# Attention stages of a two-block fp32 transformer kernel: units three deep, four gate products moved, twelve gate products per layer pair in split form

## The reference, cut to what matters

```
ga, gb, gc = the last three 1024-wide column groups of n @ w_in[i]
merged = (sigmoid(ga) * (ya @ w_branch[i, 0])
          + sigmoid(gb) * (yb @ w_branch[i, 1])
          + sigmoid(gc) * (yc @ w_branch[i, 2]))
h = h + merged @ w_out[i]
```

## Time and profile before

| | us |
|---|---|
| median of 3 runs | 3007.83 (3001.94 to 3012.53) |
| profiled execution, its own time | 3003.04 |
| its span | 3001.3 |
| PE busy | 2910.9 (97%) |
| DVE busy | 1695.5 (56%) |
| ACT busy | 1188.8 (40%) |
| mean granted PE clock | 0.983 |

### The profile page before, as it was taken

One profiled execution on the slowest core, in us unless ns is written; L12 is line 12 of the kernel. 1 busy time (PEld: TensorE's weight loads), 2 busy tenths in 40 slices (PEclk: granted clock), 3 DMA queues, 4 the chain that ended last, 5 costly groups with the idle time before them and its releaser, 6 DMA issues.

```text
span 3001.3 us, 49531 instructions
## 1 busy us (share of the span) xinstructions
PE 2910.9 (97%) x21376; PEld 2741.8 (91%) x21376; DVE 1695.5 (56%) x2824; ACT 1188.8 (40%) x1771; POOL 12.6 (0%) x20
## 2 busy tenths in 40 slices
PE   8999999999998999999999998999989999899998
PEld 8998788999998878899999996789989999678998
DVE  5666543665666553466666444456656654454665
ACT  5535422444445432244444233234454432332444
POOL 0000000000000000000000000000000000000000
PEclk9999999999999999999999898999999999999999
DMA  7544385555544344455664642445545565234553
GB/s 246 177 152 123 111 205 168 169 179 186 183 158 148 100 140 154 154 183 176 193 200 155 184 129 71 108 163 183 182 156 183 172 181 143 85 99 148 183 182 110
DMA packets 481273, 474.41 MB, mean 158 GB/s; under 512 B 47104, under 2 KB 464416, under 8 KB 480928
## 3 DMA queue, kind: packets, MB, share of 16 engines
q1 hardware_dynamic: 477472, 460.75, 49.2%
q0 software_dynamic: 3584, 10.49, 1.6%
HBM read 464.91 MB, written 6.29 MB: 157 GB/s over the span
## 4 chain that ended last, share of the span: by engine, by line
PE 92%; DVE 4%; ACT 3%; issue 1%; DMA 0%; DVEq 0%; ACTq 0%; SPq 0%
PE ps L829 33%; PE ps L928 32%; PE ps L949 17%; PE ps L982 4%; PE ps L1052 2%; PE ps L1022 1%; DVE WL L1676 1%; ACT WH L1349 1%; PE ps L872 1%; PE ps L876 1%; PE ps L880 1%; ACT REGION L1318 0%; PE ps L860 0%; DVE REGION L1819 0%; ACT L1335 0%
## 5 line engine op out<-in xcount | busy, mean ns | idle before, releaser
L1676 DVE TENSOR_TENSOR WL<-RAW,WH 128x2048 fp32r<-128x2048 f32 (+1 forms) x350 | 780.5, 2235 | 483.7 <-ACT WH L1349 481.6
L1349 ACT ACTIVATE WH<-RAW 128x2048 fp32r<-128x2048 f32 (+1 forms) x350 | 647.2, 1860 | 138.1 <-DMA RAW<-in_w_in 53.8
L949 PE MATMUL ps<-HH,WL 128*128 128x256 f32 x1408 | 394.8, 280 | 0.0
L949 PE MATMUL ps<-HH,WH 128*128 128x256 f32 x1408 | 394.3, 280 | 0.0
L949 PE MATMUL ps<-HL,WH 128*128 128x256 f32 x1408 | 394.0, 280 | 0.0
L928 PE MATMUL ps<-UH,WH 128*128 128x256 f32 x2688 | 378.5, 283 | 0.5 <-DVE WL L1676 0.5
L928 PE MATMUL ps<-UH,WL 128*128 128x256 f32 x2688 | 377.3, 283 | 0.0
L928 PE MATMUL ps<-UL,WH 128*128 128x256 f32 x2688 | 376.4, 282 | 0.0
L928 PEld LDWEIGHTS ps<-UH,WH 128*128 128x128 f32 x2688 | 346.2, 190 | 1.1 <-DVE WL L1676 0.7
L928 PEld LDWEIGHTS ps<-UL,WH 128*128 128x128 f32 x2688 | 346.7, 191 | 0.0
L928 PEld LDWEIGHTS ps<-UH,WL 128*128 128x128 f32 x2688 | 346.2, 190 | 0.0
(11 more groups left out here) (269 smaller groups left out, 3159.9 us busy)
## 6 DMA issues: line engine op xcount, KB each, us to landing
RAW<-in_w_ffn_in SPq DMA_DIRECT2D x88, 1024.0 KB, 5.1
RAW<-in_ffn_wi SPq DMA_DIRECT2D x88, 1024.0 KB, 5.1
RAW<-in_w_in SPq DMA_DIRECT2D x86, 1024.0 KB, 5.3
RAW<-in_w_ffn_out SPq DMA_DIRECT2D x32, 1024.0 KB, 5.1
RAW<-in_ffn_wo SPq DMA_DIRECT2D x32, 1024.0 KB, 5.2
RAW<-in_w_out SPq DMA_DIRECT2D x16, 1024.0 KB, 5.2
RAW<-in_w_ffn_out SPq DMA_DIRECT2D x16, 768.0 KB, 4.5
RAW<-in_ffn_wo SPq DMA_DIRECT2D x16, 768.0 KB, 4.5
```

The lines of the kernel that those rows point to most:

```text
L949: last = nc.tensor.matmul(bank(n + side, 0, T), a[:, k, side * P:(side + 1) * P], b[:, k0 + k, :], start=k0 + k == 0 and a is wh and b is ...
L1349: nc.scalar.activation(split_ap(s, part_high(s)), raw_ap(s), ACT.Copy).then_inc(weights_high, 1)
L1676: v_.tensor_tensor(split_ap(s, part_low(s)), raw_ap(s), split_ap(s, part_high(s)).bitcast(FP), ALU.subtract)\
```

## The change

Six things change together. (1) In all five attention stages PE now does the scores of unit i+3 in step i, DVE those of i+2 in its turn i, with three buffers for S, MX and SUM. (2) The last unit's transposes move ahead of the last gate product. (3) Four of C's eight gate products move between A's values and `A.out`: one before the norm's products, three behind them. (4) In mla and B the gate tiles 2 to 7 become split products: their slabs 1 to 3 are split inside the stage, in the turns 0, 2 and 4 of ACT and DVE. (5) B's split gates are first multiplied by RSTD on DVE (`gates`), which also frees the bank; ACT then takes the tanh from SBUF, and the merge waits for it (`opened`). (6) B's first gate product moves one step earlier, ahead of the second unit's scores.

```diff
+GATES_SPLIT = {"mem": 0, "mla": 1, "B": 1}
+RAW_NORM = ("B", )
+EARLY = 4
+def gate_tiles(kind, unit):
+    if kind == "C":
+        return [EARLY + unit // 2] if unit % 2 == 0 else []
+    n = DK // ATTN[kind][0]
+    return range(unit * n, (unit + 1) * n)
+def transposed(kind, step):
+    last = ATTN[kind][0] - 1
+    return [] if step < 0 or step == last else [step, last] if step == last - 1 else [step]
+def gated_unit(kind, step):
+    if step < 0:
+        return 0 if step == (-3 if kind == "B" else -2) else None
+    return step + 1 if step + 1 < ATTN[kind][0] else None
...
         attention(L + "A", "A")
+        pl.products(L + "C.early0", 1)
         pl.products(L + "A.norm", 2)
+        pl.slab_first[L + "C.early"] = len(pl.slab_last)
+        pl.products(L + "C.early1", EARLY - 1)
...
-                for i in range(-2, units):
-                    if i >= 0:
+                for step in range(-3, units):
+                    for i in transposed(kind, step):
...
-                    if i + 2 < units:
-                        for b, groups in enumerate(scores(i + 2)):
+                    if step + 3 < units:
+                        for b, groups in enumerate(scores(step + 3)):
...
-                            if kind == "mem":
+                            if m // 2 >= GATES_SPLIT.get(kind, DK):
                                 wait_split(pe, sl)
                                 terms = feature(parts(sl, DK, 256), UP, DK, cols)
```

On ACT the loop over units becomes:

```diff
+                exponentials(0)
+                exponentials(1)
+                for i in range(units):
+                    raw = kind in RAW_NORM and i > 1
+                    if i < units - 1 and not raw:
+                        gates(i)
+                    turned(i)
+                    if i + 2 < units:
+                        exponentials(i + 2)
+                    if i < units - 1 and raw:
+                        gates(i)
+                    if kind == "mem":
+                        feed.to(slab_first[name] + min(3, i + 2))
+                    elif kind in GATES_SPLIT and i in (0, 2, 4):
+                        feed.to(slab_first[name] + i // 2 + 1)
+                gates(units - 1)
```

and on DVE:

```diff
+                def gates(i):
+                    for m in gate_tiles(kind, i) if kind in RAW_NORM else []:
+                        if m // 2 >= GATES_SPLIT[kind]:
+                            wait_product(dve, f[m])
+                            v_.tensor_tensor(GATE[:, m, :], bank(f[m], 0, T), RSTD[:], ALU.mult).then_inc(evicted[f[m] % BANKS], 1)
                 scores(0)
+                scores(1)
                 for i in range(units):
-                    if i + 1 < units:
-                        scores(i + 1)
                     scale_probs(i)
+                    if i + 2 < units:
+                        scores(i + 2)
                     if i >= 1:
                         outputs(i - 1)
+                    if i < units - 1:
+                        gates(i)
                     if kind == "mem":
                         feed.to(slab_first[name] + min(3, i + 2))
+                    elif kind in GATES_SPLIT and i in (0, 2, 4):
+                        feed.to(slab_first[name] + i // 2 + 1)
                 outputs(units - 1)
+                gates(units - 1)
```

More of the change, by code:

```diff
@@ L325, in attention @@
         pl.slab_first[name] = len(pl.slab_last)
-        for m in range(1, DK, 2):
-            pl.slab(f[m * ATTN[kind][0] // DK] + m % (DK // ATTN[kind][0]), split=kind == "mem", places=places)
+        for m in range(EARLY + 1 if kind == "C" else 1, DK, 2):
+            pl.slab(f[m], split=m // 2 >= GATES_SPLIT.get(kind, DK), places=places)
         pl.products(name, n)
@@ L521, in build @@
         WIN = region(BIAS_H, T)
+        CS = region(3, 2, 16)
         PLE = MRG
@@ L574, in build @@
         blocks_ready = sem("blocks_ready")
+        opened = sem("opened")
         gelu_vec = sem("gelu_vec")
@@ L1253, in _ @@
                     product(n, [(bank(n), [(ones, AQ[:, 2 * i:2 * i + 2, :])])])
+                for m in range(1, EARLY):
+                    early_product(first[L + "C.early1"] + m - 1, slab_first[L + "C.early"] + m // 2, m)
                 tally.add("normed", 1)
@@ L1415, in attention @@
                 base = tally.add("max_ready", units)
[L1416 to L1434, removed]
-                            keys = 1 if cmp else NT if kind == "mem" else u % 2 + 1
-                            c = (1 if kind == "A" else 2) * keys * P
-                            rows = slice(0, blocks(u % 2)) if cmp else slice(0, P)
-                            evict(t[u] + b, PT[rows, b, u % 2, 0:c], bank(t[u] + b)[rows, 0:c])
-                    if i < units:
-                        if kind == "mem":
-                            feed.to(slab_first[name] + min(3, i + 2))
-                        for j in range(n_f):
-                            half_tanh(f[i] + j, GATE[:, i * n_f + j, :], bank(f[i] + j, 0, T))
@@ new lines, in exponentials @@
+                def exponentials(i):
+                    act.wait_ge(max_ready, base + i + 1)
+                    for b in range(n_b):
+                        cmp = kind == "B" and b == 0
+                        nk = blocks(i % 2) if cmp else T if kind == "mem" else (i % 2 + 1) * P
+                        nk += kind == "C"
+                        for g in range(2):
+                            dst = sums(kind, i, b, slice(0, nk))[:, g]
+                            src = bank(s[i])[:, g * T:(g + 1) * T] if kind == "mem" else dst
+                            last = nc.scalar.activation(dst, src, ACT.Exp, bias=MX[:, i % 3, b, g:g + 1],
+                                                        scale=scale, accum_out=SUM[:, i % 3, b, g:g + 1])
+                    last.then_inc(evicted[s[i] % BANKS] if kind == "mem" else exp_done, 1)
@@ new lines, in turned @@
+                def turned(i):
+                    if i >= 2:
+                        wait_product(act, o[i - 2])
+                    for b in range(n_t):
+                        cmp = kind == "B" and b == 0
+                        keys = 1 if cmp else NT if kind == "mem" else i % 2 + 1
+                        c = (1 if kind == "A" else 2) * keys * P
+                        rows = slice(0, blocks(i % 2)) if cmp else slice(0, P)
+                        evict(t[i] + b, PT[rows, b, i % 2, 0:c], bank(t[i] + b)[rows, 0:c])
@@ L1594, in _ @@
                 norm(TMP[:], TMP[:])
+                for m in range(EARLY):
+                    n = first[L + "C.early1"] + m - 1 if m else first[L + "C.early0"]
+                    half_tanh(n, early_gate(m), bank(n, 0, T))
                 attention(L + "B", "B", merged=L + "A.out")
```

100 lines of the change are left out of this document (63 added, 37 removed).

## The result

The changed kernel takes 3010.05 us (median of 20 runs, 3003.21 to 3013.29), the kernel before 3001.86 (20 runs, 2993.22 to 3012.53): a ratio of 1.0026, 95% interval 1.0017 to 1.0034, or +8 us. The forecast was 3034, +31. The sign held, the size did not. One execution of the whole study, of the run with `MX` and `SUM` grown, was in a slow state (3606.88 us at a granted clock of 0.74); the times given leave it out.

The account below looks back on a forecast made before the run. PE's work was taken as the bound, the question being whether DVE and ACT keep up with the splitting. 3003 + 11 (stages without the clock) + 20 (clock falls) = 3034 us, range 3001 to 3062.

Parts of the forecast that it names:

- The sign: Whole kernel: the change makes it slower, forecast 3034 us; chance of slower 0.72.
- Norm and C: Stretch around A's norm costs +2.4 and +1.9 us; C, losing four gates, gains 13.6 us per layer.
- A and mem: Stages without added splitting: +1.0 us in A (bounds 0 and 1.5), 0 in mem; the sum takes A +2.1.
- The stops: At transposes in mla and B, PE waits 2.3 and 2.8 us for DVE's scaling, three times per stage.
- rival (a): mla and B: splitting hidden, DVE reaches scale_probs(j+1) before PE; decided by WH starting 2.8 us earlier; 2967 us, chance 0.10.
- B's start: Start of stage B: first transposes move from 9.3 to 12.7 us behind the stage's start, +3.4 us.
- The clock: Behind the 12 new stops in mla and B the granted clock falls, costing 20 us, bounds 0 and 39.
- Sum without the clock: Whole kernel: norm +4.3, C -27.2, A +2.1, B +24.8, mla +7.0 give +11.0 us on 3003.04: 3014.
- 12 x 0.8 x 2.1 = 20 us: Clock term in mla and B: 12 new stops, 0.8 of them followed by a fall, 2.1 us each.
- rival (c): mla and B: the stops are there and the clock holds; 3014 us, chance 0.16.
- Rival (b): mla and B: the change does part of what it says, stops half as long; 2995 to 3005 us, chance 0.08.
- The rule weighed: Split products on PE: by the skill's 4 passes 0.75 of a full one, 2.59 us; prediction kept the trace's 2.88.

## Why the prediction was half right

**Norm and C: right.** 30.35 us were worked out for the stretch around A's norm, 30.11 measured, at a clock of 1.00 and without the wait. C was to lose 13.6 us per layer and lost 13.9 and 13.6. A and mem were to cost 2.1 us together (1.0 per layer in the text makes 2.0) and cost 0.3. That C's short steps need the third unit I had not weighed; the run with two, in which C takes 39.50 us, showed it.

**The stops: right in place and cause, nearly in size.** In mla they are 2.03 to 2.05 us (2.3 worked out), three per layer; in B 2.87 (2.8), but two per layer and not three, since PE comes late to the first pair. The releaser is the scaling of the probabilities, with WL just ahead of it on DVE, and the first cause is the high half on ACT behind the eviction and the exponentials: moved up by a turn, as rival (a) had its condition, the stop goes. B's start was put at 12.7 us to the first transposes and takes 13.5 and 13.8.

**The clock: right in kind, too dear.** 20 us were put down for it. The windows of one pair of B, from its even transposes to the stop, from there to the odd values, and these values:

```profile
1866.47:1876.38 9.91, 7.04 (x56) 1.00 0.30 66
1876.38:1887.04 10.66, 9.93 (x47) 0.52 0.20 39
1887.04:1889.79 2.75, 2.75 (x22) 1.00 0.00 0
```

Behind the stop the engine is at its lower level, 1.2 GHz, and then back. The pair takes 23.3 us, 20.6 by the sum without the clock, so the fall costs it 2.7. What the stages take above their sums without the clock is 2.3 us in each mla (47.09 against 41.33 + 3.5) and 4.2 and 4.3 in B (87.32 and 87.48 against 69.14 + 14.0): 13 us, not 20, and that with every other error of the sums in it. Compared with the kernel that does the same products without the stops, PE is busy 3.2 us longer in each mla (40.21 against 36.98) and 8.3 and 6.8 in B, 21.5 in all; but busy time is not time lost, since in the 10.66 us above PE waits for DVE once more in spite of the low clock. In mla the clock falls behind two of the three stops only, and a fall costs 1.5 us where 2.1 were put down. The kernel at the old addresses shows it: its first mla has one fall, its second two.

```profile
385.38:430.95 45.57, 38.67 (x281) 0.96 0.78 184
1110.27:1157.39 47.12, 40.23 (x281) 0.93 0.28 90
```

**What failed**, in the order of size:

- The step "Sum without the clock ... +11.0 us, on 3003.04, the profiled execution's own time": it took every stage that the diff does not name as it was, a term of nothing without a reason. In the profile these stages gave 14.3 us back, and the two kernels that move REGION alone put 14 to 17 us on its 64 bytes. The diff shows them only as `MX` and `SUM` with a 3 for a 2. At the old addresses the measured cost is 24.6 us, between half and all of the forecast's 31.
- The term "12 x 0.8 x 2.1 = 20 us" for the clock, which came to 13 at most. With 1.8 us of A and mem and 0.7 of norm and C that is the other 9.5 us, by which the changed stages came to +21.5 and not +31.

It is luck that rival (c), 3014, is the number nearest to the 3010 measured: it has the clock hold, and the clock fell (0.86 over B, 0.93 over mla). Rival (b), in which the stops are half as long, is wrong too.

**The rule weighed.** The Trainium skill (FP8 and Floating Point Precision, TensorE Precision Notes) gives true fp32 4 passes through the array, from which the prediction worked out 0.75 of a full product for a split one. No run here bears the 0.75 out: the split gates of mla and B take 3.03 to 3.16 us from start to start at the full clock, the full ones 3.45 to 3.65, and at the best pace seen, 113.3 ns, a split product of 24 passes would take 2.72 us (an estimate), 0.79 of 3.45. The number of passes may well hold: 3.45 us over 8 matmuls of 4 passes are 107.8 ns a pass (an estimate by that section's 4), and the traces have 113.3 to 120.0 for a pass of a split product, so that what differs is the pass.

## What to carry to other kernels

When an engine idles for the first half of a job that two engines share, look where the first half stands on the other engine's queue before giving the job up: here the place of that call was worth 42 us, the splitting itself 12. Take units deeper where a step has nothing else in it, and judge that by the stage, not by the kernel. And compare the stages that a diff does not touch before reading a time: two tiles that grew by 24 bytes each moved everything behind them, and the 14 to 17 us that this gave are more than the 8 us to be explained.

## What the runs showed of the hardware

- The pace of a split pass goes with the distance between the tile of the weights and the tile of the activations, taken modulo 256 bytes (in steps of 32 bytes): 120.0 ns at 0 and +5; 116.7 at +7 (117.9 in one stage of the kernels with six distances); 118.1 to 118.4 at +1; 117.4 to 120.1 at +3; 118.5 to 118.7 at +4; and either 113 to 114 or 117.8 at +2 and +6. Moving all tiles together by 96 bytes kept the means within 0.2. Why is open; that no distance above 256 bytes matters was not tried.
- The two paces at one distance stood in one program with the same addresses: a pass of the second half of a feed-forward stage took 113.3 ns in 7 of 8 stages and 117.8 in the other; two more programs had the shorter pace in 6 and in 5 of 8. What chooses between them is open.
- A stop of 2.0 us in mla was followed by the lower clock in some cases and not in others: four of six in the changed kernel, three of six at the old addresses and three of six with all places at multiples of 128 bytes. One of 2.9 us in B was followed by it in all twelve cases of the same three kernels; in the changed one the first of a layer held the 10.66 us behind it at a clock of 0.52, the second the 4.26 us behind it at 0.60.
